# Gate/up products of a feed-forward layer as seven half-size products instead of eight, with the weights and activations mixed on the other engines

## The reference

```python
def _swiglu(h, w_gate_up, w_down):      # h: 512 x 1024, D_FF = 2816
    gu = h @ w_gate_up                  # 1024 x 5632
    return (jax.nn.silu(gu[..., :D_FF]) * gu[..., D_FF:]) @ w_down
x = x + _swiglu(_rmsnorm(x, ffn_norm[layer]), ffn_w_gate_up[layer], ffn_w_down[layer])
```

## Time and profile before

| what | value |
|---|---|
| median of 3 runs | 1297.76 us (1297.55 to 1297.77) |
| span of the profiled execution, first to last instruction | 1294.5 us |
| PE matmuls busy | 1282.6 us, 6525 instructions |
| PE weight loads busy | 1028.3 us |
| DVE, ACT, POOL busy | 561.9, 551.6, 611.3 us |
| granted TensorE clock, mean | 0.999 of full speed |
| HBM read, written | 119.15 MB, 6.29 MB |

### The profile page before, as it was taken

How to read it: one execution, slowest core, us unless ns; L and a number is a source line. 1 busy time by engine, 2 the same in 40 slices (tenths; PEclk the granted TensorE clock), 3 DMA queues, 4 the chain that set the end, 5 groups by cost and what they waited for, 6 DMA issues and landing times.

```text
span 1294.5 us, 18372 instructions
## 1 busy us (share of the span) xinstructions
PE 1282.6 (99%) x6525; PEld 1028.3 (79%) x6525; DVE 561.9 (43%) x872; ACT 551.6 (43%) x1006; POOL 611.3 (47%) x487
## 2 busy tenths in 40 slices
PE   8999999999999999999999999999999999999998
PEld 6877787877778888888888887777888888888886
DVE  4855666666535512121202056999843131311011
ACT  5454454445435433333323247785533233333223
POOL 4565664646535454545444453430444444444442
PEclk9999999999999999999999999999999999999999
DMA  6522222222233333333332345224323333343322
GB/s 210 160 73 62 68 68 58 66 57 67 89 97 111 96 98 97 97 96 94 102 95 85 106 126 175 66 68 152 98 82 91 104 90 105 89 122 98 97 95 93
DMA packets 123415, 126.31 MB, mean 98 GB/s; under 512 B 7896, under 2 KB 106456, under 8 KB 122712
## 3 DMA queue, kind: packets, MB, share of 16 engines
q1 hardware_dynamic: 123320, 125.46, 32.3%
q10 hardware_dynamic: 32, 0.01, 0.0%
HBM read 119.15 MB, written 6.29 MB: 97 GB/s over the span
## 4 chain that ended last, share of the span: by engine, by line
PE 65%; issue 19%; POOL 10%; DVE 3%; ACT 2%; DMA 1%; POOLq 0%; SPq 0%; ACTq 0%; DVEq 0%
PE ps L1518 19%; PE ps L1520 18%; PE ps L1519 18%; POOL w_lo L502 10%; PE ps L1896 2%; PE ps L1613 1%; PE ps L1625 1%; PE ps L1636 1%; PE ps L1671 1%; PE ps L1648 1%; PE ps L1652 1%; PE ps L1682 1%; PE ps L1690 1%; DMA x_tok<-in_x_dram 1%; DVE gelu_g L1426 0%
## 5 line engine op out<-in xcount | busy, mean ns | idle before, releaser
L502 POOL TENSOR_TENSOR w_lo<-w_stage,w_hi 128x512 fp32r<-128x512 f32 (+2 forms) x430 | 545.6, 1274 | 667.5 <-ACT w_hi L562 667.2
L562 ACT ACTIVATE w_hi<-w_stage 128x512 fp32r<-128x512 f32 (+2 forms) x448 | 264.5, 594 | 569.6 <-PE ps L1520 551.7
L1518 PE MATMUL ps<-h_hi,w_hi 128*128 128x512 f32 x1104 | 439.7, 398 | 1.7 <-DVE h_lo L955 1.0
L1520 PE MATMUL ps<-h_hi,w_lo 128*128 128x512 f32 x1104 | 430.5, 390 | 0.0
L1519 PE MATMUL ps<-h_lo,w_hi 128*128 128x512 f32 x1104 | 430.4, 390 | 0.0
L1518 PEld LDWEIGHTS ps<-h_hi,w_hi 128*128 128x128 f32 x1104 | 207.4, 188 | 61.1 <-issue 14.2
L1520 PEld LDWEIGHTS ps<-h_hi,w_lo 128*128 128x128 f32 x1104 | 207.3, 188 | 43.7
L1519 PEld LDWEIGHTS ps<-h_lo,w_hi 128*128 128x128 f32 x1104 | 207.5, 188 | 43.2 <-issue 2.6
L1301 DVE TENSOR_TENSOR silu_g<-ps,rstd_wide 128x512 f32<-128x512 f32 x44 | 30.2, 686 | 327.5 <-PE ps L1520 327.5
L1518 PE MATMUL ps<-w_hi,f_hi 128*128 128x512 f32 x176 | 68.7, 390 | 0.1
L1519 PE MATMUL ps<-w_lo,f_hi 128*128 128x512 f32 x176 | 68.5, 389 | 0.0
(11 more groups left out here) (229 smaller groups left out, 1634.3 us busy)
## 6 DMA issues: line engine op xcount, KB each, us to landing
w_stage<-in_ffn_w_gate_up_dram SPq DMA_DIRECT2D x176, 256.0 KB, 3.1
w_stage<-in_ffn_w_down_dram SPq DMA_DIRECT2D x88, 256.0 KB, 2.7
w_stage<-in_even_w_in_dram SPq DMA_DIRECT2D x96, 192.0 KB, 2.5
w_stage<-in_odd_w_in_dram SPq DMA_DIRECT2D x32, 256.0 KB, 2.8
x_spill<-x_t SPq DMA_DIRECT2D x2, 2048.0 KB, 8.6
x_t<-x_spill SPq DMA_DIRECT2D x2, 2048.0 KB, 9.3
w_stage<-in_odd_w_out_dram SPq DMA_DIRECT2D x16, 256.0 KB, 2.8
w_stage<-in_even_w_out_dram SPq DMA_DIRECT2D x16, 192.0 KB, 2.4
```

The lines of the kernel that those rows point to most:

```text
L502: pool.tensor_tensor(out=w_lo[:, s, 0:n], in0=stage[:, s, 0:n], in1=w_hi[:, s, 0:n].bitcast(f32), op=ALU.subtract).then_inc(chunk_lo, 1)
L562: act.activation(w_hi[:, j % RING, 0:n], stage[:, j % RING, 0:n], ACT.Copy).then_inc(chunk_hi, 1)
L1518: pe.matmul(out_, lh, rh, start=start, stop=False, skip_group_check=skip)
L1520: return pe.matmul(out_, ll, rh, start=False, stop=stop, skip_group_check=skip)
```

## The change

The first group of each layer stays. The other ten, 20 tile pairs, become 20 units of one pair each. A unit treats one gate tile and one up tile as a 2 x 2 block product: rows are gate (g) and up (u), the inner dimension is split into features 0-511 (1) and 512-1023 (2), the tokens into two halves of 256. Eight half-size products would be needed; Strassen's scheme, in Winograd's form, takes seven:

- weights: p1 takes g1, p2 takes g2, p4 takes u2 as they are; p5 takes u1+u2, p6 that minus g1, p3 g2 minus p6's, p7 g1-u1. DVE makes these four sums (`w_add`) in `w_sum`.
- activations: p1, p2, p3 use quarters of h; p5, p6, p7, p4 use four mixtures of quarters (`h_mix`), made once per layer while the first group runs: ACT scales x by the gain (`gained`), DVE does 4 x 4 subtractions (`mix_sums`), ACT the high parts (`mix_high`), DVE the low parts (`mix_low`).
- outputs: gate, early tokens = p1+p2; gate, late = (p1+p6)+p5+p3; up, late = (p1+p6+p7)+p5; up, early = p1+p6+p7+p4. p1, p6, p7 and p4 add into one bank, which is read by others between the products; p2 and p3 share a second bank, p5 has a third. The first one alternates between two banks from unit to unit.

Each product is 4 inner tiles x 3 = 12 matmuls of 256 columns and takes one slot of the ring of four. The raw weights come as four 256 KB tiles per unit, double-buffered by unit, in rows of 128 floats (512 bytes) where the chunks had rows of 256. The low parts of p5 and p7 are made by DVE, those of the other five by POOL. 1/rms is no longer applied to up but to the product f (`f_scale`). f is kept in float32 and split into high and low twice, once for each half of the down projection. The banks of the first group and of the down projection are exchanged to suit, `softplus_out` (a chain of small DVE operations for the recurrent block) moves from the start of layer 0's block into its down projection.

```diff
+def unit_products(u):
+    first = [("p4", u - 1)] if u else []
+    return [("p1", u)] + first + [(name, u) for name in ("p2", "p5", "p6", "p3", "p7")]
+PRODUCTS = [step for u in range(UNITS) for step in unit_products(u)] + [("p4", UNITS - 1)]
+DVE_LOWS = ("p5", "p7")
...
         # SP, ffn_loads(n)
-                with sync.Fori(0, GATE_GROUPS) as i:
-                    group(i, 0)
+                def raw_chunks(u):
+                    for name in ("u1", "u2", "g1", "g2"):
+                        if u == 0:
+                            sync.wait_ge(chunk_used, c0)
+                        elif u == 1:
+                            sync.wait_ge(chunk_lo, c0 + PLAIN_CHUNKS)
+                        else:
+                            raw_free(u - 2, name)
+                        dst = raw_tile(u, name).rearrange("p (k f) -> p k f", k=4)
+                        k0, at_ = 512 * (name[1] == "2"), P * (2 * PLAIN + u)
+                        sync.dma_start(dst, w_gu[n][k0:k0 + 512, int(name[0] == "u"), at_:at_ + P].rearrange("(k p) f -> p k f", p=P))\
+                            .then_inc(raw_in[u % 2][RAW_SLOT[name]], 16)
...
         # POOL
+                for name, u in PRODUCTS:
+                    if name not in DVE_LOWS:
+                        product_low(n, name, u)
...
         # ACT, second_half and ffn
+                gained(0)
+                operand(n // 2, 6)
+                gained(1)
+                mix_high(0)
+                gained(2)
+                operand(n // 2, 7)
+                mix_high(1)
+                gained(3)
+                mix_high(2)
+                operand(n // 2, 8)
+                mix_high(3)
                 act.activation(scratch[:, n:n + 1], ones[:, 0:1], ACT.Sqrt)
                 root(n)
...
+                for e in range(5, len(PRODUCTS)):
+                    product_high(n, e)        # waits for product e - 4
+                    name, u = PRODUCTS[e]
+                    if name == "p5":
+                        silu(2 * PLAIN + u - 1)
+                    if name == "p6":
+                        first_copy(u)
+                    if name == "p1":
+                        fifth_copy(u - 1)
+                    if u == last and name in ("p6", "p3"):
+                        f_high(int(name == "p3"))
...
         # DVE, ffn
+                mix_sums(0)
+                mix_sums(1)
+                mix_low(0)
                 if n == 1:
                     x_to_tokens(0)
+                mix_sums(2)
+                mix_low(1)
+                if n == 1:
                     x_to_tokens(1)
+                mix_sums(3)
+                mix_low(2)
+                if n == 1:
                     x_to_tokens(2)
+                late_rms(nn)
+                mix_low(3)
+                if n == 1:
                     x_to_tokens(3)
+                for name in UNIT_SUMS:        # p5, p6, p3, p7
+                    w_add(name, 0)
+                plain_gates()
+                for u in range(UNITS):
+                    if u:
+                        late_up(u - 1)
+                    w_low("p5", u)
+                    if u:
+                        unit_f(u - 1)
+                    if u == 0:
+                        plain_f()
+                    early_gate(u)
+                    w_add("p5", u + 1)
+                    w_add("p6", u + 1)
+                    if u == UNITS - 1:
+                        f_scale(0)
+                        f_scale(1)
+                    w_low("p7", u)
+                    late_gate_part(u)
+                    w_add("p3", u + 1)
+                    if u == UNITS - 1:
+                        f_scale(2)
+                        f_low(0)
+                    late_gate(u)              # and the gate scaling in place
+                    w_add("p7", u + 1)
+                f_scale(3)
+                f_low(1)
+                late_up(UNITS - 1)
...
+                for i in range(4, KF + RING):
+                    f_scale(i + 2)
+                    f_low(i)
+                    if i == KF // 2 and n == 0:
+                        softplus_out()
...
         # PE, multiply(name, u)
+                    if name in DVE_LOWS:
+                        pe.wait_ge(product_lo_dve, N_DVE_LOWS * n + LOW_COUNT[name, u])
+                    else:
+                        pe.wait_ge(product_lo, N_POOL_LOWS * n + LOW_COUNT[name, u])
...
+                    if name == "p2" and u:
+                        pe.wait_ge(outs_combined, combined(n, u - 1, 3))
+                    if name == "p5":
+                        if u == 0:
+                            pe.wait_ge(mix_lo_done, 4 * (n + 1))
+                        else:
+                            pe.wait_ge(fifth_out, UNITS * n + u)
+                    if name == "p6":
+                        pe.wait_ge(first_out, UNITS * n + u + 1)
+                    if name in ("p3", "p7", "p4"):
+                        pe.wait_ge(outs_combined, combined(n, u, {"p3": 1, "p7": 2, "p4": 4}[name]))
+                    x = {"p1": 0, "p6": 0, "p7": 0, "p4": 0, "p2": 1, "p3": 1, "p5": 2}[name]
+                    for k in range(4):
+                        rh, rl = tokens_of(name, k)
+                        last = mm3(unit_bank(u, x), w_hi[:, s, k * P:(k + 1) * P], w_lo[:, s, k * P:(k + 1) * P], rh, rl,
+                                   name in ("p1", "p2", "p3", "p5") and k == 0, k == 3, True)
+                    last.then_inc(product_done, 1)
```

More of the change, by code:

```diff
@@ L801, in _, with ffn @@
                     square(1, (0, 2, 3)[i - 16], (2, 3, 5)[i - 16], G_FFN)
[L803 removed]
+            def ffn(n, nn, next_gain, fb):
                 c0 = C_FFN[n]
[L806 to L815, removed]
[L816 to L831 removed]
@@ new lines, in ffn @@
+                second_half(nn, gain, c0, gained, mix_high)
+                for e in range(1, RING):
+                    product_high(n, e)
+                silu(0)
+                silu(1)
+                first_copy(0)
+                product_high(n, RING)
+                last = UNITS - 1
+                for e in range(5, len(PRODUCTS)):
+                    product_high(n, e)
+                    name, u = PRODUCTS[e]
+                    if name == "p5":
[6 more added lines that the diff above has]
+                        f_high(int(name == "p3"))
@@ new lines, in ffn @@
+                first = c0 + PLAIN_CHUNKS
+                fifth_copy(last)
+                f_high(2)
+                conv(first)
+                f_high(3)
+                conv(first + 1)
+                silu(KF - 1)
+                f_high(4)
+                conv(first + 2)
+                f_high(5)
+                conv(first + 3)
+                for d in range(RING, 2 * KF):
+                    f_high(d + 2) if d + 2 < 2 * KF else None
+                    conv(first + d)
+                    if d == KF + RING - 1:
+                        if next_gain is None:
+                            for c in range(NC):
+                                y_square(c)
+                        else:
+                            square(nn + 1, 0, 4, next_gain)
@@ L1267, in finish @@
                     y_sum(0, c)
+                for i in range(KF + RING, KF + RING + 4):
+                    f_low(i)
                 dve.wait_ge(y_squared, NC)
@@ L1792, in ffn, with plain_group @@
                 c0 = C_FFN[n]
-                def group(it, half, wait=True, first=False):
-                    b0 = 4 - fb if half else fb
-                    if wait:
-                        pe.wait_ge(f_ready, it * 4 + (KF * n + 2 * half - 2))
+                def plain_group():
                     for k in range(KD):
-                        j = half * KD + k
-                        if first and k == NORM_SUM_AT:
+                        c = c0 + k
+                        if k == NORM_SUM_AT:
@@ L1813, in ffn @@
                 pe.wait_ge(x_new, 2 * KD + 4 if n else 5)
-                group(0, 0, wait=False, first=True)
+                plain_group()
                 pe.wait_ge(rstd_wide_ready, nn)
@@ L1817, in ffn @@
                     pe.wait_ge(x_tok_in, NC)
[L1818 to L1837 removed]
+                for name, u in PRODUCTS:
+                    multiply(name, u)
```

512 lines of the change are left out of this document (361 added, 151 removed).

## The result

The changed kernel takes 1346.36 us (median of 4 runs, 1345.72 to 1347.53) against 1297.65: ratio 1.038 [1.0366, 1.0396], 48.7 us slower. Forecast was 1336 in a range of 1284 to 1360. The profiled execution's span is 1345.7, 51.2 above that of before; it was the slowest of the four (1347.53), and the spans lie 2.5 us further apart than the medians.

The account below looks back on a forecast made before the run. The matmul array, busy 99% of the span, was taken as the bound. Products -36.0, unit stalls +47.1, stage start +19 and stage end +8 gave +38 us: forecast 1336 us, range 1284 to 1360.

Parts of the forecast that it names:

- Part 1: Products in the gate/up stage: 1680 matmuls of 256 columns replace 960 of 512 per layer, -36.0 us in two layers.
- Part 2: Other engines' work per unit: each fits alone, but DVE and POOL share a port used 9.9 of 10.0 us.
- Alternation: DVE and POOL take turns at the SBUF port with both queues full: 0.56 us for DVE, 1.14 for POOL.
- Part 3: Wait before p4 in units 1 to 19: stall of 1.24 us, period 11.24 us, +47.1 us in all.
- Part 4: Start of the stage, where the first group must cover h's mixing: +8.2 us layer 0, +11 layer 1, together +19.
- Part 5: End of the stage, last unit: p3 1.3 us late, p4(19) directly after p7; +4 us per layer, 8 in two.
- The 3.3 us: Time from the profiled span of 1294.5 us to the median of 1297.76, outside first and last instruction, taken to stay.
- DVE keeps the port: Rival: DVE keeps the port at the gate scaling, 4.65 us into the unit; `late_up` on time, -8 us, 1290; chance 0.20.
- DVE is the bound: Rival: in the units each POOL operation is waited for once, 12.4 us per unit, 1380 us; chance 0.11.
- Half of the units stall: Rival: only half of the units have the stall, or it is half as long; 1313 us; chance 0.10.

Follow-up runs that it names:

- experiment 1: Changed kernel with DVE's sum for the next unit's p7 moved from ahead of `late_up` to behind it: 1309.21 us, ratio to before 1.010.
- experiment 7: As experiment 1, with the units' gate scaling also reading 1/rms from an idle PSUM bank, copied there by ACT: 1298.93 us, ratio to before 1.002.
- experiment 3: Changed kernel without the mixing of h; p5, p6, p7 and p4 read a plain quarter of h: 1327.01 us, ratio to before 1.023.
- experiment 6: Changed kernel with the last unit's `late_up` first and its f highs behind the weight highs: 1338.2 us, ratio to before 1.032.
- experiment 5: Changed kernel with ACT's square root and DVE's reciprocal ahead of the fourth quarter's mixing: 1343.42 us, ratio to before 1.036.

## Why the prediction was right

**Part 1.** The pitch holds: 0.120 over long stretches where eleven pitches of the earlier trace rows gave 0.119. That thousandth, over 3360 matmuls, and a chunk of 2.72 against 12 x 0.227 make -32.0 of the forecast -36.0: 4 us too much gain. The weight loads stayed hidden, as said. The Trainium skill's gap of 109 ns for 256 columns (TensorE: Matmul & The Clock Gate, section Back-to-back issue gap) does not fit: the products' usual distance is 120 ns. The estimate from it for the products, 47.5 us, would have been 15.5 too high.

**Part 2.** Alternation held, with 0.55 and 1.16 where I had 0.56 and 1.14. The claim of 9.9 of 10.0 us at the port was the most useful one: experiments 1 and 7 show a port with too little slack (10.36) and one with room (10.08). In the units DMA cost nothing, no wait there names one; at the start of layer 0's block the trace says otherwise (part 4).

**Part 3.** The place, the queue and the size were right: p4, behind `late_up`, behind the sum for p7, which waits for POOL's low of p2. POOL's lows take 1.52 to 1.65 us on average, at the upper end of the 1.4 to 1.6 named and a little over it. The stall against full pitches is 1.22 (forecast 1.24), the period 11.30 (11.24). It occurs 18 times per layer and not 19, because in the first unit p7 is late instead and p4(0) then is not: 43.9 against 47.1.

**Part 4.** +19.2 against +19, but that it is so close is luck. I expected 5 us before the first p1 of layer 0 and 3 before p5, and they are 7.9 and 0.6, with 2.1 before p7(0) that I had not seen; in layer 1 the delay before the transposes was right in kind, and all of the start comes to 8.6 against 11. In layer 0 the reciprocal starts at 429.96 and not at 426.5, because the mixing began late. My walk took over from the kernel before that DVE is free at 411.2 (its last `h_lo` at 409.44). Here that `h_lo` came at 413.10, since ACT had to write the high part of the group's fifth chunk before the square and high of the last part of x, and the chunk had not landed. ACT before and after, and DVE's first sum of the mixing:

```profile
406.19 0.61 ACT L562 ACTIVATE w_hi<-w_stage 128x512 fp32r<-128x512 f32 x1
...
410.61 0.63 ACT L723 ACTIVATE w_hi<-w_stage 128x512 fp32r<-128x512 f32 x1 [4.42 <-DMA w_stage<-in_ffn_w_gate_up_dram]
...
414.80 1.51 DVE L1551 TENSOR_TENSOR h_sum<-h_gained 128x256 f32<-128x256 f32 x1
```

SP issues the four raw tiles of unit 0 ahead of that chunk, which so went out at 405.10 (before: at 401.55). In experiment 3 ACT waits as long for it (4.13 us) and p1 for nothing, so it costs only through the mixing behind it. No run moved these loads; that they explain the 3.5 us is read from the traces and not shown by an experiment.

**Part 5.** +9.2 against +8; experiment 6 made the kernel 8.2 faster, by 6.1 in waits and the rest through the clock.

**What was missing** is the clock. I had named a lower clock in the gaps as something not counted; it is about 9 us and most of the distance from +38 to +48.7. The kernel before has no half-speed stretch until its end, so no row could price it, but the direction was plain: PE at 99% hides that a wait costs more than its length. Without it the sum comes to +40; the misses of the other parts (+4 in part 1, -3 in part 3, +1 in part 5) leave +2. The 3.3 us that I put outside the span are 1.8 to 2.1 in every run for which both times are listed; the forecast does not depend on it, since it adds to the median.

**The rivals.** *DVE keeps the port* fell at the point named: the sum at 560.88 was held until POOL was through. My row against alternation was read too quickly, and the line in the earlier trace rows beside POOL's operation is a matmul. The DVE row that I meant stands in the same timeline of the kernel before:

```profile
818.17 0.68 DVE L1408 TENSOR_TENSOR i_g<-i_g,m_g 128x512 f32<-128x512 f32 x1
818.78 1.21 DVE L1414 TENSOR_TENSOR_SCAN r_g<-a_g,i_g 128x512 f32<-128x512 f32 x1
```

POOL's operation of 3.23 us came from 6.69 us of rest into a running row of DVE operations. There DVE did go first, twice; whether an engine that comes from rest is treated otherwise was not tried. Between two full queues they alternated in every unit. *DVE is the bound* fell too: experiment 1 gives 37 us back with all of DVE's work in place. *Half of the units stall*: 18 of 20 did.

## What to carry to other kernels

Where VectorE and GpSimd both have work with SBUF operands, add up the port and not the engines: here 9.9 of 10.0 us of port, where the windows of the stage show DVE busy 78% and POOL 71%, waits at the port included. In front of an operation that frees a bank for the matmul array put none that needs the port, and take an operand that is used again and again (here 1/rms) from PSUM instead. When loads are put ahead of others in a list, look at what stands behind those others on every engine. Fewer matmuls pay only if what they wait for at the seams is worked out too, and a wait of several us on the matmul array is to be priced with a few us at half speed behind it.

## What the hardware showed that I had not expected

- In or behind waits of PE of 2 to 8 us the granted clock fell to half for 3.4, 6.8 or 10.2 us; not behind every one (the gaps of 1.27 us never did it; the wait of 2.2 us before p7(0) was followed by a drop in layer 0 but not in layer 1 of the changed kernel, and the other way round in experiments 5 and 6). Idle matmuls in the wait kept it at the full level.
- Time at the port is listed as busy time: DVE shows 163.0 us of 180 in experiment 1 and 141.1 in experiment 7 for the same operations, 22 us of queueing.
